# A one-core decoder block: rows of four experts chosen at once, two experts placed at once, a shorter warm chain in the routing

## What is computed

```python
def route(xf, w_router, b_router):              # xf: 512 x 1024
    s = sigmoid(xf @ w_router)                  # 32 experts in 8 groups of 4
    sel = s + b_router
    grp = sum of the top 2 of sel in each group
    best group per token, then the top 2 experts in it
    return e_idx, w / sum(w)                    # w: s at the two experts

def expert_block(xb, e):                        # rows of the tokens that chose e
    h = silu(xb @ w_gate[e]) * (xb @ w_up[e])   # 1024 -> 512
    return h @ w_down[e]                        # 512 -> 1024

x = layer_norm(ALPHA * x + y)                   # y: each token's two experts, weighted
```

## Time and profile before

| | us |
|---|---|
| median of 3 runs (1108.92 to 1110.22) | 1109.71 |
| the profiled execution's own time | 1108.49 |
| its span in the profile | 1106.7 |
| TensorE products, busy | 1070.9 (97%) |
| VectorE, ScalarE, GpSimd, busy | 356.4, 266.7, 38.3 |
| read from memory | 249.2 MB |

### The profile page before, as it was taken

The page is one execution under the profiler, slowest core; times in us unless marked ns, Lnnn a source line. Parts: engine busy times, 40 slices in busy tenths (PEclk is TensorE's granted clock), DMA queues, the critical chain, the costliest instruction groups (busy, mean ns, idle before and its releaser), DMA issues.

```text
span 1106.7 us, 16406 instructions
## 1 busy us (share of the span) xinstructions
PE 1070.9 (97%) x6806; PEld 551.1 (50%) x6806; DVE 356.4 (32%) x817; ACT 266.7 (24%) x537; POOL 38.3 (3%) x86
## 2 busy tenths in 40 slices
PE   8999999999898999999999999999999999999995
PEld 4444455557655554566544844444444444444442
DVE  0179623234655645203216311212121121202122
ACT  2431122234435520013401111212112121212121
POOL 2000100000000000100000100000000000000000
PEclk9999999999999999999999999999999999999998
DMA  8012320211122150553333899999999999999970
GB/s 277 24 61 76 115 77 2 78 49 49 60 77 84 72 191 1 179 238 120 154 124 119 341 401 422 422 420 421 420 420 406 420 416 417 418 412 421 409 302 9
DMA packets 51229, 252.41 MB, mean 228 GB/s; under 512 B 5329, under 2 KB 6481, under 8 KB 26321
## 3 DMA queue, kind: packets, MB, share of 16 engines
q1 hardware_dynamic: 47616, 246.05, 56.0%
q0 software_dynamic: 2304, 4.20, 1.0%
q10 hardware_dynamic: 1232, 1.07, 0.3%
HBM read 249.21 MB, written 6.29 MB: 231 GB/s over the span
## 4 chain that ended last, share of the span: by engine, by line
PE 53%; issue 4%; DVE 1%; ACT 0%; POOL 0%; POOLq 0%; ACTq 0%; DVEq 0%
PE cpair L1973 19%; PE bank L1983 9%; PE tpair L1996 6%; PE bank L2042 3%; PE bank L1805 2%; PE bank L1785 2%; PE bank L1961 2%; PE tpair L1805 1%; PE bank L1778 1%; PE cpair L1805 1%; PE tpair L1785 1%; PE cpair L1785 1%; PE cpair L1887 1%; PE tpair L1827 1%; PE bank L2020 1%
## 5 line engine op out<-in xcount | busy, mean ns | idle before, releaser
L1973 PE MATMUL cpair<-ring,xgT 128*64 128x512 f32 x496 | 130.7, 592 | 0.0
L2398 DVE COPY hT<-bank 128x256 f32<-128x256 f32 x32 | 13.6, 425 | 330.2 <-PE bank L1962 330.2
L1973 PEld LDWEIGHTS cpair<-ring,xgT 128*64 128x64 f32 x496 | 41.8, 137 | 70.4 <-issue 70.3
L1996 PEld LDWEIGHTS tpair<-sel,xgt 128*128 128x128 f32 x256 | 60.9, 328 | 10.7 <-issue 10.6
L2198 ACT ACTIVATE hs<-cpair 64x512 f32<-64x512 f32 x32 | 18.9, 589 | 188.8 <-PE cpair L1973 188.8
L1996 PE MATMUL tpair<-sel,xgt 128*128 128x128 f32 x256 | 64.0, 404 | 0.0
L922 PE MATMUL bank<-xT,ring 128*128 128x512 f32 x128 | 60.9, 606 | 0.0
L365 PE MATMUL bank<-xT,ring 128*128 128x512 f32 x112 | 48.5, 593 | 0.0
L1983 PE MATMUL bank<-ring,hT 128*64 128x512 f32 x208 | 47.8, 598 | 0.0
L2204 ACT ACTIVATE ye<-bank 128x512 f32<-128x512 f32 x32 | 19.0, 593 | 111.9 <-PE bank L1983 111.9
L2042 PE MATMUL bank<-ye,combT 64*128 64x512 f32 x128 | 41.7, 629 | 0.7 <-ACT ye L2204 0.7
(11 more groups left out here) (425 smaller groups left out, 1759.0 us busy)
## 6 DMA issues: line engine op xcount, KB each, us to landing
ring<-in_w_exp_gate SPq DMA_DIRECT2D x31, 1024.0 KB, 9.9
ring<-in_w_exp_up SPq DMA_DIRECT2D x31, 1024.0 KB, 9.9
ring<-in_w_exp_down SPq DMA_DIRECT2D x26, 1024.0 KB, 9.9
ring<-in_w_in SPq DMA_DIRECT2D x6, 2048.0 KB, 8.1
ring<-in_w_mem_kv SPq DMA_DIRECT2D x4, 2048.0 KB, 10.0
xT<-in_w_exp_down SPq DMA_DIRECT2D x7, 1024.0 KB, 10.8
avq<-in_w_exp_down SPq DMA_DIRECT2D x7, 1024.0 KB, 9.8
mixT<-in_w_exp_gate SPq DMA_DIRECT2D x6, 1024.0 KB, 11.2
```

Of the source, the lines that this page charges most:

```text
L1973: last = nc.tensor.matmul(bank[b][m * CAP:(m + 1) * CAP, :], x(h, j), w(m, h)[:, j * DE:(j + 1) * DE], start=(k == 0), stop=(k == KT - 1))
L1996: last = nc.tensor.matmul(tpair[:, h, k * P:(k + 1) * P], xgt[:, g % 2, h * 512 + k:(h + 1) * 512:KT // 2], sel[:, :, :].rearrange("p e c ...
```

## The change

1. `chosen(g, r)` picks for the four experts of a group at once: `sel` is 128 x (4 x 64), a bank holds 2 products of 256 columns instead of 4 of 128, and `xgT` holds four experts. It takes two calls a group, r = 0 and r = 1, 4 products each; the first stands where the old call stood (before `down` of the group's third expert), the second behind that `down`. The calls for experts 2, 3 of each group are gone.
2. `combined(p)` places two experts at once, with 128 stationary rows, at every second expert: `ye` and `combT` hold both experts' rows one above the other, so ScalarE copies each expert's result in two pieces of 64 partitions (63 pieces; the last is VectorE's), and `selg` is made in two halves.
3. `placing(e)`, the table that VectorE makes for `placing_turned(e)`, is made in expert e's own turn and no longer one ahead; `selg` and `hT` have one buffer.
4. The five counts of unread products go from 20, 5, 10, 4, 14 to 10, 4, 4, 0, 6.
5. To free memory, the gates that only the slower loop reads move into `lists` and are stored to `gates_kept` in memory; the load of piece 21, into `lists`, waits for that store too.

```diff
-UNREAD = (20, 5, 10, 4, 14)
+UNREAD = (10, 4, 4, 0, 6)
...
+        vals = lists_at[:, 1100:1356].rearrange("p (t f e) -> p t f e", t=NT, f=2)
+        gates_kept = nc.dram_tensor("gates_kept", (P, NT, NE), F32, kind="Internal").ap()
...
                     load_piece(sp, NPL - 3)
+                    sp.wait_ge(vals_done, 1)
+                    sp.dma_start(gates_kept, vals[:, :, 1, :]).then_inc(gates_out, 16)
                     sp.wait_ge(tabs_done, 1)
                     load_piece(sp, NPL - 2)
                     sp.wait_ge(more_known, 1)
+                    sp.wait_ge(gates_out, 16)
                     load_piece(sp, NPL - 1)
...
-                    def chosen(p):
-                        g = 2 * p // EPG
-                        pe.wait_ge(sel_done, 2 * p + 2)
+                    def chosen(g, r):
+                        pe.wait_ge(sel_done, EPG * (g + 1))
                         pe.wait_ge(xg_here[g % 2], 16 * (g // 2 + 1))
-                        if p:
-                            pe.wait_ge(x_read, 2 * p)
-                        for h in range(2):
-                            for k in range(KT // 2):
-                                last = nc.tensor.matmul(tpair[:, h, k * P:(k + 1) * P],
-                                                        xgt[:, g % 2, h * 512 + k:(h + 1) * 512:KT // 2],
+                        for b in range(2):
+                            n = 4 * g + 2 * r + b
+                            if n >= 2:
+                                pe.wait_ge(x_read, n - 1)
+                            for i in range(2):
+                                k = 2 * b + i
+                                last = nc.tensor.matmul(tpair[:, b, i * EPG * CAP:(i + 1) * EPG * CAP],
+                                                        xgt[:, g % 2, r * 512 + k:(r + 1) * 512:KT // 2],
                                                         sel[:, :, :].rearrange("p e c -> p (e c)"), start=True, stop=True)
                             last.then_inc(x_full, 1)
...
-                    def combined(e):
-                        i, g = e % EPG, e // EPG
-                        pe.wait_ge(y_read, e + 1)
-                        pe.wait_ge(comb_read, e + 1)
+                    def combined(p):
+                        i, g = p % 2, p // 2
+                        pe.wait_ge(y_read, 4 * p + 4)
+                        pe.wait_ge(comb_read, 2 * p + 2)
...
-                            last = nc.tensor.matmul(bank[6 + h][:, :], combT[half[h], e % 2, :], ye[half[h], e % 2, :],
-                                                    start=(i == 0), stop=(i == EPG - 1))
+                            last = nc.tensor.matmul(bank[6 + h][:, :], combT[:, h, :], ye[:, h, :],
+                                                    start=(i == 0), stop=(i == 1))
                         last.then_inc(c_done, 1)
...
-                        if e >= 2:
-                            combined(e - 2)
-                        if e % 2 and e < LAST:
-                            chosen((e + 1) // 2)
+                        if e % 2 and e >= 3:
+                            combined(e // 2 - 1)
+                        ends = e % EPG == EPG - 1 and e < LAST
+                        if ends:
+                            chosen(e // EPG + 1, 0)
                         if e:
                             down(e - 1)
+                        if ends:
+                            chosen(e // EPG + 1, 1)
                     placing_turned(LAST)
                     hidden(LAST)
-                    combined(LAST - 1)
                     down(LAST)
-                    combined(LAST)
+                    combined(pairs - 1)
...
                     def rows_read(e):
                         act.wait_ge(w_read, read_at[e, DN, 1])
                         if e >= 2:
-                            act.wait_ge(c_done, e - 1)
-                        nc.scalar.activation(ye[:, e % 2, :], bank[5][:, :], ACT.Copy).then_inc(y_read, 1)
+                            act.wait_ge(c_done, e // 2)
+                        for h in range(1 if e == LAST else 2):
+                            s = half[h ^ e % 2]
+                            nc.scalar.activation(ye[s, h, :], bank[5][s, :], ACT.Copy).then_inc(y_read, 1)
...
+                    def placing(n):
+                        if n:
+                            dve.wait_ge(comb_full, n)
+                        for s in range(2):
+                            e = n // 2 * 2 + (s ^ n % 2)
+                            V.tensor_scalar(selg[:, s * CAP:(s + 1) * CAP], caps, table[:, 0, e:e + 1],
+                                            table[:, 1, e:e + 1], ALU.is_equal, ALU.mult).then_inc(selg_done, 1)
```

More of the change, by code:

```diff
@@ L1560, in block_of, with further_blocks @@
                 eng.wait_ge(out_rows[s], 16 * NGRP // 2)
-        def further_blocks(eng, body, after):
+        def further_blocks(eng, body, after, before=None):
             eng.wait_ge(more_known, 1)
@@ L1568, in further_blocks @@
                 block_of(eng)
+                if before:
+                    before()
                 with eng.Fori(1, n + 1) as blk:
@@ L1639, in experts, with before @@
                         load_piece(sp, n)
+                    def before():
+                        sp.dma_start(gates_back, gates_kept).then_inc(f_gates, 16)
                     def body(blk):
@@ L1659, in after @@
                         sp.wait_ge(f_done, 16 * NT)
-                    further_blocks(sp, body, after)
+                    further_blocks(sp, body, after, before)
                     block_of(sp)
@@ L1976, in gate_up_terms, with down_terms @@
                         return last
-                    def down_terms(ht, w, h):
+                    def down_terms(ht, w, h, odd=0):
                         for j in range(FT // 2):
@@ L2217, in root @@
                             .then_inc(rooted, 1)
-                    chosen(0)
+                    chosen(0, 0)
+                    chosen(0, 1)
                     for e in range(NE):
                         silu(e)
-                        if e % 2 and e < LAST:
-                            chosen((e + 1) // 2)
+                        ends = e % EPG == EPG - 1 and e < LAST
+                        if ends:
+                            chosen(e // EPG + 1, 0)
                         if e >= EPG and e % EPG == 1:
@@ L2440, in experts @@
                         hidden(e)
-                        if e < LAST:
-                            placing(e + 1)
-                        if e % 2 == 0 and e + 2 < NE:
-                            select(e // 2 + 1)
+                        if e:
+                            placing(e)
+                        if e % EPG == 0 and e + EPG < NE:
+                            select(e // EPG + 1)
                         if e >= EPG and e % EPG == 1:
```

105 lines of the change are left out of this document (55 added, 50 removed).

## The result

The changed kernel took **1100.13 us** in the median of 4 runs (1098.87 to 1101.06); the kernel before took 1109.97 us beside it (4 runs, 1108.92 to 1111.37). The ratio is 0.991, with a 95% interval from 0.9893 to 0.9927: 0.9% faster, where 1.5% and 1093.0 us were predicted. The sign is right, the size is not, and the time lies above the range. The profiled execution took 1099.95 us, with a span of 1098.2.

What follows compares the result with a forecast made beforehand. TensorE was taken as the bound, 14.65 us behind the weight stream. Piece 187 landing at 1061.1 plus an end of 29.55 gave span 1090.65; with 1.8 and 1.2 added, 1093 us. Range 1089 to 1098.5, 8 in 10.

Steps and rivals of the forecast that it cites:

- The bound: Expert stage: TensorE bounds the kernel before; after the change the stream of weight pieces decides.
- the reserve: At the second half of the last `gate_up`, TensorE runs 14.65 us behind the weight stream; a faster TensorE can take that.
- the end: From piece 187's landing to the end of the span: 27.85 us as before plus small additions, 29.55 us.
- The sum: Adds the terms: 26.9 us off TensorE's path, about 12.9 paid out, the stream deciding, span 1090.65, time 1093 us.
- The routing: Before the experts: fewer unread products start the first choice 3.9 us earlier, `gate_up(0)` and piece 22 3.6 us earlier.
- Rival 1: Low clock during the first choice and half of `gate_up(0)`: 3.4 to 5 us more, 1096 to 1098 us; 20%.
- Rival 4: The routing gives 0 since the gather lands late among the weight pieces: 1096.6 us; 5%.
- the clock at 0.5 for more than two short stretches: Sign in the profile after that would show the prediction wrong: TensorE's granted clock at half speed that often.
- nothing is won: Even experts: `combined` goes, but `down` starts no earlier, as it waits for the copy of `hT`.
- idle between pieces for over a microsecond an expert from about expert 22: Sign in the profile after that would confirm the forecast: TensorE waiting in the expert stage while the stream stays full.
- The dearer end for a choice: Choice for four experts: strided weight loads don't overlap products, so 5.7 us in place of 3.9.
- The store: Gates' store on SP's queue: costs zero; at its dear end piece 21 leaves 3 us later, still ahead of piece 22.

Runs made afterwards that it cites:

- e3: Changed kernel with one of the eight depth steps of gate and up left out for experts 1 to 31, all weights still loaded: 1100.51 us, ratio 0.9924.
- e7: Kernel before with only the five new counts of unread products (10, 4, 4, 0, 6): 1110.05 us, ratio 1.0002.
- e9: Changed kernel with the store of the gates issued first and piece 19 held until the first gather has landed: 1097.27 us, ratio 0.9888.
- e11: Changed kernel once more, unchanged: 1099.62 us, ratio 0.9906.
- e10: Changed kernel with 20 unread products and not 6 behind the table's, filling the wait for the gather: 1098.70 us, ratio 0.9901.
- e4: Kernel before with one of the eight depth steps of gate and up left out for experts 1 to 31: 1098.84 us, ratio 0.9914.
- e2: Changed kernel without the store of the gates and without the wait for it: 1100.57 us, ratio 0.9929.
- e5: Changed kernel with piece 19 and all behind it on SP's queue, the gates' store included, held until the first gather has landed: 1098.09 us, ratio 0.9901.
- e1: Changed kernel with the five old counts of unread products (20, 5, 10, 4, 14): 1099.09 us, ratio 0.9918.
- e6: As e5, with the counts of unread products set to 12, 5, 5, 2, 12: 1098.31 us, ratio 0.9901.
- e12: The same kernel as e9, run once more: 1098.97 us, ratio 0.9894.

## Why the prediction was right and wrong

**The bound, the reserve and the end: right.** The stream took over from TensorE, as the chain and e3 show. The end behind piece 187 was forecast at 29.55 us and took 29.8. The sum had "about 12.9" paid out of the 26.9 us taken off the path of TensorE; that is the part behind T alone, 42.5 - 29.55, and 12.7 were paid. By the sum's own terms 3.1 us of an earlier stream were to come on top, to 1090.65, and these did not come: T was 4.2 us later than before instead. The stream's rate of 2.53 us a piece became 2.54.

**The routing: wrong, and this is the step that failed.** The prediction had the gather land "4.5 later", "at about 624.5", and the first choice 3.9 us earlier, so that piece 22 would go at 632.5. Up to the request its working holds: less the 1.4 of t0 the ranks and the gather's request came as worked out (619.98, where 619.95 was forecast). The table's products came 0.9 later than worked out (623.78 less 1.4, against 621.4), in a stretch at the lower clock; it cost nothing, since `sel` was still ready before the gather. But the gather landed 8.1 us after its request, so the choice began at 629.61 and not at 624.6: 1.4 from t0, 3.6 from the landing. From the choice to piece 22 it took 9.2 us in place of 7.9, 1.3 for the clock. In sum 6.3 us. The 4.5 was a duration of the profile of before, and I carried it over as if it belonged to the gather. It belonged to the moment: e7 moved nothing but that moment, and 4.5 became 7.7. The profile of before could have said so. Its six later gathers, asked while the pieces ran without a hole, took 8.3 to 8.7 us each; the 8.7 stands in the earlier trace rows, and the prediction used it for the groups' rows but not for the first gather. In e9, where the gather has its room again, piece 22 goes 25.9 us after t0; the forecast's 632.5 is 24.7 after the t0 of before, and the 1.2 between them are the landing of 5.7 against 4.5. The prediction's way of counting holds there, and only that term doesn't.

**The rivals.** Rivals 1 and 4 happened together. Rival 1 had named the clock in the first choice, "3.4 to 5 us more"; from the start of the choice to piece 22 it cost 1.3 in this profile and 2.3 in e11's, and e10 gives 0.9 of it back, so the price was too high. Rival 4 had named the gather that "lands late among the weight pieces" at 5%, and that was the larger part, 3.6. Rival 1 was said to end at 1096 to 1098, rival 4 at 1096.6. That they can add up, and that the stream may start later than before and not only as late, was in none of the cases, and so the range ended at 1098.5. One of the signs of being wrong came too, the clock at 0.5 for more than two short stretches: it was there from 620 to 624, in the first choice and in the last `gate_up`.

**What was mis-sized beside it.** The stream from piece 22 to T took 429.5 and not 428.1 + 0.5: 1.0 more. e4 has the like of it without the change (429.8); its cause stays open. With 0.25 at the end the span's miss is complete: 6.3 + 1.0 + 0.25 = 7.55 = 1098.2 - 1090.65. From the span to the median I had added 1.8 + 1.2; it was 1.75 + 0.2. The 1.2 very likely stood for the early t0 in the profile of before, which the profile of after did not have, so that 1.05 of the 1.4 us of t0 were already in the sum. So 7.55 - 1.05 leaves 6.5, and with the 0.6 by which I had rounded 1092.4 + 1.2 down to 1093 the miss is the 7.1 us between 1093 and 1100.13.

**TensorE's pace: a little too hopeful, without effect.** From 740.31 to 965.15 are 16 experts, 14.05 us each, 56.2 for a group of four; before it was 2 x 29.06 = 58.1, and the prediction makes it 58.1 - 3.93 + 0.65 + 0.5 = 55.3. A choice for four cost 4.25 and not 3.9, and `combined` 0.88 more than before at each odd expert, not 0.65 or 0.5; at even ones `down` starts 0.5 behind `hidden` (718.34 to 718.84) and not 1.03, which was "nothing is won" in the prediction and is a gain. So TensorE met the stream later than at expert 22: the chain leaves it for the transfers at 994.51, in `gate_up(26)`, and it first waits for a piece in `gate_up(29)`. It was 3.6 us ahead by its waits for pieces, and 5.3 with the 1.7 that the last `gate_up` took longer at the lower clock, not 9. It was enough, but the sign "idle between pieces for over a microsecond an expert from about expert 22" did not come. The dearer end for a choice, 5.7 us, is out at the full clock. The Trainium skill ("TensorE: Matmul & The Clock Gate", Part 3, The mechanism) lets a load overlap a running product only in another row group; 0.27 us for a record of 256 columns at full height is less than the sum of 0.12 and 0.236, so the trace doesn't follow that rule here.

**The store: right.** I took it at zero, with a dear end at which piece 21 leaves 3 us later than its 628.62. It landed 8.1 us after its issue, and piece 21 left at 631.46, 2.8 later: the dear end. From t0 that is 1.4 later than before and 4.0 later than in e2, and e2 shows that it costs the time nothing as long as the routing is late anyway. In e5, where the routing is no longer late, the same store is what remains, and e9 gains by moving it.

What stays open: the choice for four and the placing of two were not run apart from each other. e3 says that behind the stream neither can show in the time; how much of TensorE's relief each of them is comes from the chain alone.

## What to carry to other kernels

The landing time of this gather was not a property of the transfer alone; it told how full the engines were when it came. Before moving a small transfer that something waits for, look at the DMA share in the two or three microseconds around it, before and at its new place, and at what is issued beside it; let the small ones go first and the bulk wait for them. Later transfers of the same kind in the same profile give the price in the crowd. And where a faster engine uncovers a stream, the stream's end is the sum to make: less work elsewhere pays once, up to the reserve, and then not at all.

## What the hardware showed that I had not expected

**A gather shares with the pieces around it.** The same gather landed in 4.5 us in a stretch with a DMA share of 0.79 (4.6 in e4), in 7.4 to 8.5 us with pieces close around it (0.95 to 1.03 from 620 to 624 in after and e7), and in 5.4 to 5.7 us when the pieces behind it were held back. In these last its packets still waited for 3.0 us behind the request, and the six later gathers of the kernel before waited 3.5 to 4.3 us for their first packet. The Trainium skill ("DMA: Bandwidth & Descriptors", Queues, rings and completion order) says that an engine takes turns between its queues a packet at a time; the runs agree in that another queue's pieces slow the gather down, by 2 to 3 us between its first packet and its landing, though no run here shows the packets' order, and turns alone don't explain the wait for the first packet.

**The clock behind a wait.** The first choice, 16 records of 256 columns, took 4.19 to 4.27 us where TensorE had waited 0 to 1.63 us ahead of it (e1, e5, e6, e9, e10), and 5.60 to 6.58 us, behind waits of 1.96 to 3.64 (after, e2, e3, e11, e12), with the granted clock at 0.50 to 0.67 where I read it by stretches of 2 us (after, e11, e12), that is at 1.2 and not 2.4 GHz for most of it. The old choice, 16 records of 128 columns, hardly feels this: in e7 it took 4.07 us behind a wait of 2.68, with the clock at 0.65 and then 0.50, against 3.89 at full speed, and its weight loads took 3.81 us in both. The clock was also down from 620 to 624 in after, e7 and e9, where TensorE was busy without a gap, with products and with loads; from 612 to 620 it had idled for at most 0.4 us at a time. The gather was asked 12.2 us after t0 in them as in e5, where it stayed at full speed; only the table came later, 14.6 us after t0 in after and 13.6 in e5, and nothing waited for it.

**A low clock can be free.** In the changed kernel the first half of the last `gate_up` ran at a granted clock of 0.53 to 0.62 (1064 to 1068), 8.78 us for the whole and not the usual 7.04, but piece 187 landed at 1068.4 anyway, and the second half was through at 1072.19, 3.8 later. The timeline of TensorE:

```profile
1063.48 8.78 PE L1984 MATMUL cpair<-ring,xgT 128*64 128x512 f32 x32 [2.13 <-DMA ring<-in_w_exp_up]
...
1072.19 0.33 PE L2032 MATMUL bank<-ident,selg 128*128 128x128 f32 x1
```
